# Norm sums in strips of 32 rows, low-rank norms inside the input product, queries rotated per head, attention values for 256 queries at once

## The reference

```python
def rms_norm(x, g):
    xf = x.astype(jnp.float32)
    y = xf * lax.rsqrt(jnp.mean(xf * xf, axis=-1, keepdims=True) + EPS)
    return (y * g.astype(jnp.float32)).astype(x.dtype)
# a layer of the first block, l = 0, 1
hx = modulate(rms_norm(x, norm1_g[l]), sh1, sc1)      # and hc for the context
px = hx @ w_in[l]                                     # 384 q rank, 256 kv rank, 32 rope, 256 fourier, 768 hyena
q  = (rms_norm(px[:, :384], q_norm_g) @ w_uq)         # 8 heads of 64 + 32 (the 32 are rotated by position)
kv = (rms_norm(px[:, 384:640], kv_norm_g) @ w_ukv)    # 8 heads of 64 keys + 64 values
prob = softmax((q_nope k_nope + q_rope k_rope) * scale); o = prob @ v
x = x + g1 * (concat[o, fourier, hyena] @ w_out[l])
x = x + g2 * sq_relu_mlp(modulate(rms_norm(x, norm2_g[l]), sh2, sc2), w_mlp1[l], w_mlp2[l])
```

## Time and profile before

| | us |
|---|---|
| median of 3 runs | 3166.07 (3163.94 to 3166.35) |
| the profiled execution | 3160.84 |
| its span in the trace | 3158.9 |
| mean granted clock of TensorE | 0.946 |
| PE busy | 2836.2 (90%) |
| PE weight loads | 2315.9 (73%) |
| DVE busy | 1645.4 (52%) |
| ACT busy | 1164.0 (37%) |

### The profile page before, as it was taken

The page is one execution under the profiler, slowest core; times in us unless marked ns, Lnnn a source line. Parts: engine busy times, 40 slices in busy tenths (PEclk is TensorE's granted clock), DMA queues, the critical chain, the costliest instruction groups (busy, mean ns, idle before and its releaser), DMA issues.

```text
span 3158.9 us, 43981 instructions
## 1 busy us (share of the span) xinstructions
PE 2836.2 (90%) x16708; PEld 2315.9 (73%) x16708; DVE 1645.4 (52%) x2656; ACT 1164.0 (37%) x2158; POOL 376.3 (12%) x583
## 2 busy tenths in 40 slices
PE   5889789998788897799979999999899986997899
PEld 3636568886646896588758888877688863975799
DVE  3432554334534664587247777774544433358665
ACT  3224242223323543333245445552422223332443
POOL 0000000000000000000026666660000000014000
PEclk8999899999998999899979999999999987999899
DMA  6136122222343455622400000022222247210354
GB/s 245 67 123 237 40 80 93 93 93 80 115 174 129 156 182 224 263 94 95 145 14 1 1 2 1 1 94 84 76 102 98 93 174 275 81 67 1 121 186 146
DMA packets 49600, 343.13 MB, mean 109 GB/s; under 512 B 5296, under 2 KB 7344, under 8 KB 9776
## 3 DMA queue, kind: packets, MB, share of 16 engines
q1 hardware_dynamic: 44960, 324.03, 27.8%
q10 hardware_dynamic: 4496, 17.15, 1.4%
HBM read 333.82 MB, written 7.34 MB: 108 GB/s over the span
## 4 chain that ended last, share of the span: by engine, by line
PE 83%; DVE 7%; ACT 4%; DMA 3%; issue 2%; DVEq 0%; POOL 0%; ACTq 0%; SPq 0%; POOLq 0%
PE ps L514 18%; PE ps L515 18%; PE ps L516 18%; DMA ring<-in_w_dram 3%; PE ps L1848 3%; PE ps L1835 3%; PE ps L1827 2%; PE ps L1856 2%; PE ps L697 1%; PE ps L542 1%; PE ps L689 1%; PE ps L720 1%; PE ps L563 1%; DVE ring_rest L502 1%; PE ps L1790 1%
## 5 line engine op out<-in xcount | busy, mean ns | idle before, releaser
L514 PE MATMUL ps<-hidden_high,w_high 128*128 128x256 f32 (+1 forms) x1160 | 385.5, 332 | 11.8 <-DVE h_rest L510 8.7
L514 PE MATMUL ps<-h_high,w_high 128*128 128x512 f32 (+1 forms) x1024 | 349.2, 341 | 29.9 <-DVE h_low L1377 26.3
L515 PE MATMUL ps<-h_low,w_high 128*128 128x512 f32 (+1 forms) x1024 | 348.0, 340 | 0.0
L999 ACT ACTIVATE w_high<-ring 128x2048 fp32r<-128x2048 f32 x124 | 236.8, 1909 | 295.0 <-PE ps L516 295.0
L515 PE MATMUL ps<-hidden_low,w_high 128*128 128x512 f32 (+1 forms) x1024 | 342.9, 335 | 0.0
L2166 POOL TENSOR_SCALAR RS<-C,arena 128x128 f32<-128x128 f32 x128 | 74.9, 604 | 1635.2 <-DVEq L1750 1635.2
L516 PE MATMUL ps<-hidden_high,ring_rest 128*128 128x256 f32 (+1 forms) x872 | 262.8, 301 | 0.0
L514 PEld LDWEIGHTS ps<-hidden_high,w_high 128*128 128x128 f32 x1160 | 218.2, 188 | 37.0 <-issue 10.7
L514 PEld LDWEIGHTS ps<-h_high,w_high 128*128 128x128 f32 x1024 | 196.0, 191 | 54.4 <-issue 33.0
L1329 DVE SCALAR_TENSOR_TENSOR X<-ps,M,X 128x256 f32<-128x256 f32 x240 | 106.6, 479 | 218.3 <-PE ps L516 218.3
L515 PEld LDWEIGHTS ps<-h_low,w_high 128*128 128x128 f32 x1024 | 196.2, 192 | 20.8
(11 more groups left out here) (400 smaller groups left out, 6312.3 us busy)
## 6 DMA issues: line engine op xcount, KB each, us to landing
ring<-in_w_dram SPq DMA_DIRECT2D x302, 1024.0 KB, 4.8
z_spill<-arena ACTq DMA_DIRECT2D x16, 256.0 KB, 2.0
arena<-z_spill SPq DMA_DIRECT2D x2, 2048.0 KB, 9.6
C<-in_first_dram ACTq DMA_DIRECT2D x1, 2432.0 KB, 8.8
X<-in_x_dram ACTq DMA_DIRECT2D x1, 2048.0 KB, 13.2
x_spill<-X ACTq DMA_DIRECT2D x1, 2048.0 KB, 8.4
X<-x_spill SPq DMA_DIRECT2D x1, 2048.0 KB, 7.6
C<-in_third_dram ACTq DMA_DIRECT2D x1, 2048.0 KB, 14.8
```

Source lines behind the costliest of these rows:

```text
L514: ins = nc.tensor.matmul(out_, w_high, high, start=first, stop=False)
L515: nc.tensor.matmul(out_, w_high, rest, start=False, stop=False)
L999: nc.scalar.activation(W_HIGH[:, (j + 1) % 2, :], ring[:, s], ACT.Copy).then_inc(sems["w_high"], 1)
```

## The change

Five edits:

1. **Sums in strips.** pe_sums no longer multiplies 512 (or 256) columns by 128 x 128 ones. The tokens are cut into four quarters; quarter q is multiplied by 128 x 32 ones in column group q, and its sums land on partitions 32q to 32q+31 of the first T/4 columns of the bank. Root and reciprocal work on 128 x T/4. Then PE spreads the reciprocals back: four matmuls with 32 x 128 ones, one for each strip, into banks 4 to 7 (the ones' 32 rows add 32 equal values, so the root is taken of 1024 times the mean). DVE scales straight from these four banks. In the modulation stages the spread stands behind the last slab.
2. **Low-rank norms within the input product.** The stage is gone. ACT squares the five tiles after its copy of slab 3, PE adds them in strips behind slab 3's filter matmuls, ACT takes two roots after its copy of slab 4, DVE two reciprocals after its copy of slab 4, PE spreads behind slab 4 into banks 0 to 3 (and waits there for both reciprocals), DVE scales the five tiles and rotates the key part after its copy of slab 5. The filter's length moves from tile 14 to 15, and the last slabs' tiles to 13, 20 and 22.
3. **Queries turned per head**: DVE rotates head h as soon as it is out of PSUM, within the query product.
4. **Attention values for 256 queries.** Units go head by head, both query blocks of a head together. DVE takes the reciprocal of each unit's sum and scales its exponentials before they are turned. For each pair of units PE makes one product with the values as weights (128 columns, two heads) and 256 moving columns; DVE copies the 64 rows of the head into MIX. The turning of the output by PE and ACT's copy of it are gone.
5. PT becomes two buffers of 4 x 256, OR is gone, and new small buffers lie in the arena.

```diff
-            nc.tensor.matmul(ps[:, b, 0:T], ones[:], RS[:, 0, 0:T], start=True, stop=False)
-            nc.tensor.matmul(ps[:, b, 0:T], ones[:], square_of(KD - 1)[:, 0:T], start=False, stop=True).then_inc(filled[b], 1)
+            pe_strips(ps[:, b, :], [RS[:, 0, :], square_of(KD - 1)], T).then_inc(filled[b], 1)
+
+        def pe_strips(to, terms, T):
+            w = T // 4
+            for n, x in enumerate(terms):
+                for q in range(4):
+                    ins = nc.tensor.matmul(to[32 * q:32 * q + 32, 0:w], ones[:, 0:32], x[:, q * w:(q + 1) * w], start=(n == 0), stop=(n == len(terms) - 1),
+                                           tile_position=(0, 32 * q))
+            return ins
+
+        def pe_spread(pe, v, x, first, w, nth):
+            for q in range(4):
+                pe.wait_ge(freed[first + q], v.free(first + q, nth[q]))
+                ins = nc.tensor.matmul(ps[:, first + q, 0:w], ones[32 * q:32 * q + 32, :], x[32 * q:32 * q + 32, 0:w], start=True, stop=True)
+            ins.then_inc(sems["spread"], 1)
+
+        def pe_factors(pe, v, nth, T):
+            pe.wait_ge(sems["root"], v.of("root", 1))
+            pe_spread(pe, v, RS[:, 0, :], 4, T // 4, nth)
...
-            nc.scalar.activation(RS[:, 0, 0:T], ps[:, b, 0:T], ACT.Sqrt, bias=eps[:], scale=1.0 / D).then_inc(freed[b], 1)
+            nc.scalar.activation(RS[:, 0, 0:T // 4], ps[:, b, 0:T // 4], ACT.Sqrt, bias=eps32[:], scale=1024.0 / D).then_inc(freed[b], 1)
-            nc.vector.reciprocal(RS[:, 0, 0:T], RS[:, 0, 0:T]).then_inc(dve_step, v.step())
-            dve.wait_ge(dve_step, v.steps())
+            nc.vector.reciprocal(RS[:, 0, 0:T // 4], RS[:, 0, 0:T // 4]).then_inc(sems["root"], 1)
-            nc.vector.tensor_tensor(H[:, k, 0:T], X[:, k, 0:T], RS[:, 0, 0:T], ALU.mult).then_inc(sems["scaled"], 1)
+            if k == 0:
+                dve.wait_ge(sems["spread"], v["spread"])
+            nc.vector.tensor_tensor(quarters(H[:, k, 0:T], T), quarters(X[:, k, 0:T], T), factors(T), ALU.mult).then_inc(sems["scaled"], 1)
...
+        def pe_lora(pe, v, l, j):                      # called after slab j's matmuls and filter
+            if j == 3:
+                b = LORA_SUMS % 8
+                pe.wait_ge(freed[b], v.free(b, LORA_SUMS // 8))
+                pe.wait_ge(sems["squares"], v.of("squares", 5))
+                for n, (first, terms) in enumerate(((0, 3), (3, 2))):
+                    ins = pe_strips(ps[:, b, n * P:n * P + P], [LSQ[:, first + k, :] for k in range(terms)], lora_tokens(l, n))
+                ins.then_inc(filled[b], 1)
+            if j == 4:
+                pe.wait_ge(sems["root"], v.of("root", 3))
...
+            if j == 4:                                 # dve_lora, after the copy of slab 4's second tile
+                nc.vector.reciprocal(LRT[:, 0, 0:T // 4], LRT[:, 0, 0:T // 4]).then_inc(sems["root"], 1)
+                nc.vector.reciprocal(LRT[:, 1, :], LRT[:, 1, :]).then_inc(sems["root"], 1)
...
             for h in range(HEADS):                     # dve_up
-                dve.wait_ge(freed[h], v.freed(h))
-            for h in range(HEADS):
+                if h % 2:
+                    dve.wait_ge(filled[h], v.filled(h))
+                    nc.vector.tensor_scalar(QT[:, h, 0:T], ps[:, h, 0:T], -SCALE, None, ALU.mult).then_inc(freed[h], 1)
+                dve.wait_ge(freed[h], v.freed(h))
                 nc.vector.tensor_tensor(RT[64:96, h, :], QT[96:128, h, 0:L], C[96:128, 0:L], ALU.mult).then_inc(dve_step, v.step())
...
+                if 1 <= i <= n:                        # dve_attn
+                    u = i - 1
+                    dve.wait_ge(freed[u % 2], v.freed(u % 2, u // 2 + 1))
+                    nc.vector.reciprocal(ST[:, 3, u:u + 1], ST[:, 1, u:u + 1]).then_inc(dve_step, v.step())
+                    dve.wait_ge(dve_step, v.steps())
+                    nc.vector.tensor_scalar(PR[:, u % 3, 0:kn], PR[:, u % 3, 0:kn], ST[:, 3, u:u + 1], None, ALU.mult).then_inc(sems["scaled"], 1)
...
+                if 3 <= i < n + 3 and i % 2 == 0:      # pe_attn
+                    s, h, q = units[i - 3]
+                    pair, hp = (i - 4) // 2, h // 2 * P
+                    for a in range(kn // P):
+                        ins = nc.tensor.matmul(ps[:, b, 0:L], VT[:, k0 // P + a, hp:hp + P], PT[:, pair % 2, a, :], start=(a == 0), stop=(a == kn // P - 1))
```

More of the change, by code:

```diff
@@ L316, in build @@
         KA = part(12288, 2, 256)
+        LSQ = part(12800, 5, T2)
+        LRT = part(15360, 2, P)
+        KRT = part(15616, L)
         RK = part(29056, 8)
@@ L618, in pe_filter, with lora_tokens @@
                 ins.then_inc(filled[b], 1)
+        def lora_tokens(l, n):
+            return T2 if l == 0 or n == 1 else L
+        def pe_lora(pe, v, l, j):
[8 more added lines that the diff above has]
+                pe.wait_ge(sems["root"], v.of("root", 3))
+                for n in range(2):
+                    w = lora_tokens(l, n) // 4
+                    for q in range(4):
+                        pe.wait_ge(freed[q], v.free(q, 2))
+                        ins = nc.tensor.matmul(ps[:, q, n * P:n * P + w], ones[32 * q:32 * q + 32, :], LRT[32 * q:32 * q + 32, n, 0:w], start=True, stop=True)
+                    ins.then_inc(sems["spread"], 1)
         def pe_in(pe, v, l):
@@ L625, in pe_in @@
                 pe_filter(pe, v, l, j)
+                pe_lora(pe, v, l, j)
             v.end(U_IN)
[L627 to L631, removed]
-            T = T2 if l == 0 else L
-            for b, (k0, n, tok) in enumerate(((0, 3, T), (3, 2, T2))):
-                pe.wait_ge(freed[b], v.free(b))
-                for k in range(n):
-                    pe.wait_ge(sems["squares"], v.of("squares", k0 + k + 1))
-                    ins = nc.tensor.matmul(ps[:, b, 0:tok], ones[:], H[:, k0 + k, 0:tok], start=(k == 0), stop=(k == n - 1))
-                ins.then_inc(filled[b], 1)
-            v.end(U_LORA)
             pe.drain().then_inc(pe_stage_end, 1)
@@ L925, in act_attn @@
         def act_attn(act, v, l):
-            units, m, through = attn_units(l), len(woven(l)), turned_woven(l)
+            units, m = attn_units(l), len(woven(l))
             n = len(units)
-            for i in range(n + 4):
+            for i in range(n + 2):
                 if i < n:
@@ L1225, in dve_attn, with out_of @@
         def dve_attn(dve, v, l):
-            units, slabs, through = attn_units(l), woven(l), turned_woven(l)
+            units, slabs = attn_units(l), woven(l)
             n, m = len(units), len(slabs)
-            for i in range(n + 3):
+            def out_of(pair):
+                s, h, q = units[2 * pair]
+                b, r = 4 + pair % 2, 64 * (h % 2)
+                dve.wait_ge(filled[b], v.filled(b, pair // 2))
+                nc.vector.tensor_copy(MIX[r:r + 64, h // 2, s * L:(s + 1) * L], ps[r:r + 64, b, 0:L]).then_inc(freed[b], 1)
+            for i in range(n + 4):
                 if i < n:
@@ L1416, in build @@
         U_READ = {**{b: 3 for b in (2, 3, 4, 6)}, 7: 2, 5: 2, "h_high": 16, "h_split": 16}
-        U_DOUT = {**banks(9), "slab": 8, **U_SUMS, "w_high": 8, "w_split": 8}
+        U_DOUT = {**banks(9), "spread": 1, "root": 1, "slab": 8, **U_SUMS, "w_high": 8, "w_split": 8}
         DIRS = (0, 1)
```

202 lines of the change are left out of this document (89 added, 113 removed).

## The result

The changed kernel takes 3084.99 us (median of four executions, 3075.03 to 3090.59) against 3165.59 us before: ratio 0.9749, 95% interval 0.9728 to 0.9771, 80.6 us less. A second comparison gave 3084.17 against 3163.86 us, 0.9749 with 0.9736 to 0.9762. The forecast was 3097.6 us with a range of 3082 to 3116: sign and range hold, the size was 12.6 us too small.

The account below looks back on a forecast made before the run. PE was taken as the bound (busy 2836 of 3158.9 us), gains being its pauses and low clock. Terms -33.2 + 9.2 - 4.0 - 22.4 - 14.5 - 3.5 = -68.4 from 3160.84 gave 3092.4, as median 3097.6; range 3082 to 3116.

Parts of the forecast that it names:

- Low-rank stage gone, work put into the input product: Between input and query product: removing the norms' own stage gains 33.2 us in two layers; their work inside costs 9.2.
- the wait behind slab 4: Input product: PE waits for DVE's copy and two reciprocals before slab 5, costing 2.0 us in layer 0, 1.3 in layer 1.
- Clock behind it: Query product: without the long pause before it PE keeps its clock, -4.0 us over two layers (bounds 0 and -5).
- Rotation: Query rotation hidden beside the query product: attention starts 10.0 us earlier per layer, plus 1.2 of clock each, together -22.4.
- The 1.3 us a head for PE in layer 1: Layer 1 query product: PE needs 1.3 us a head, so DVE's rotation falls back a few us and catches up later.
- Nine norms: Block norms in strips: shorter sums, roots and reciprocals less a new spread, -14.5 us in all (bounds -5 and -19).
- The spread's 0.75: Block norms: PE's eight instructions spreading the reciprocals back were taken at 0.75 us, between 1.0 one by one and 0.35 overlapped.
- the first rival: Spreads overlap in row groups (0.35 instead of 0.75 us) and strips are cheap (1.3): 3092 us, chance 0.2.
- Attention: Attention stage: turning gone (-3.4), values product +0.2 a layer, small gains and costs at the ends, sum -3.5 (bounds -7 and +5).
- attention steps over 4 us: Attention: a sign that would show the prediction wrong; right would be steps of 3.5 us with no 4.5 among them.
- +1.0 for the units and -1.0 for the tail: Layer 0's attention end: last eight units without a slab cost 1.0 us for DVE's work; the shorter tail gains 1.0.
- the fourth rival, attention as a chain: Attention: PE's transposes wait for DVE's minimum, reciprocal and scaling, 1.6 us in each of 48 units, +77, so 3174; chance 0.03.

Follow-up runs that it names:

- the best one: Changed kernel plus value products of two heads at a time, low-rank reciprocals ahead of slab 4's copy and an early one-column root: 3062.87 us, ratio 0.9684.
- the head pairs: Changed kernel with value products of two heads at a time, each with 64 weight columns in its own column half: 3075.52 us, ratio 0.9722.

## Why the prediction was right, and where it was off

- *Low-rank stage gone, work put into the input product* (-33.2 + 9.2 = -24.0): measured -24.8. Terms inside were off and cancel. The spreads and strips are cheaper than put (0.66 and 1.2 us in layer 0, against 1.2 and 1.7), and the wait behind slab 4 was 1.67 us against 2.0: slab 5 starts 66.0 us behind the stage's first product where it was 62.8, 3.3 us later instead of 4.9. But in eight of nine profiles the clock falls behind that wait, which the sum had at 0: 1.6 us in slabs 5 and 6.
- *Clock behind it* (-4.0): -4.5, the windows at 1.00 instead of 0.59.
- *Rotation* (-22.4): -19.95 and 1.9 of clock. The hand-over of 0.15 us was right. The 1.3 us a head for PE in layer 1 is not what the earlier trace rows give (12.83 / 8 = 1.6, part of it at the low clock); the changed kernel's 10.53 us for eight heads bear it out.
- *Nine norms* (-14.5): the seven on the path gave -19.0 by stages, where they were put at -15.3; undoing the nine cost 15.5 by medians. This is the mis-sized term. The start gained 4.9 against 4.0, the one behind layer 0's output product 3.0 against 2.7, the two of 512 tokens behind MLP and delta 3.35 and 3.42 against 3.1, the three of 256 tokens 4.4 against 2.4 together. From the start of the reciprocal to the first scale the seven gave 8.8 us, where the sum had 13.2 for the reciprocals less seven times 0.85 for spread and hand-over, some 7.2. The spread's 0.75 was too dear: it took 0.45 to 0.51 at the full clock, though 0.69 to 0.81 where the clock was low. The rest of the excess lies in the sums: from the first sum to the root the 256-token norms took 1.1 to 2.1 us in the kernel before, the longer ones at least in part at the low clock, and 0.5 to 1.2 with strips. On the spread the first rival was right, at a chance of 0.2; its 3092 was still 7 us high.
- *Attention* (-3.5): 1.2 to 1.35 by stages, nothing by medians. The turning went as said. The sign "attention steps over 4 us" came up and meant no harm: with one product for two units the steps are 2.66 and 4.40 us, 3.53 on average. Half of what is missing is in the last eight units of layer 0: from the first of their scores to the Fourier stage 15.97 us before, 17.1 now (256.18 to 273.25), where +1.0 for the units and -1.0 for the tail had been put. There two units take 3.0 us, 1.5 each where they took 1.3, and no engine is busy throughout:

```profile
261.14 0.43 DVE L1257 COPY arena<-ps 64x256 f32<-64x256 f32 x1 [0.91 <-PE ps L751]
261.60 0.42 DVE L1264 TENSOR_REDUCE arena<-ps 128x1 f32<-128x256 f32 x1
261.94 0.15 DVE L1269 RECIPROCAL arena<-arena 128x1 f32<-128x1 f32 x1
262.13 0.35 DVE L1271 TENSOR_SCALAR arena<-arena 128x256 f32<-128x256 f32 x1
262.40 0.42 DVE L1264 TENSOR_REDUCE arena<-ps 128x1 f32<-128x256 f32 x1
...
264.18 0.41 DVE L1257 COPY arena<-ps 64x256 f32<-64x256 f32 x1 [0.91 <-PE ps L751]
```

  DVE waits 0.91 us for PE's product before it copies, and then scales the exponentials of the next unit, for which PE waits in turn (0.41 to 0.87 us, L740). This is the fourth rival, attention as a chain, in the eight units that have no slab to fill PE's steps; elsewhere it did not come. The other half, some 0.6 us in layer 1 and the rest in layer 0, was not located.
- *What the sum did not have*: 13.4 us outside its terms. 4.4 are the two Fourier stages, where the kernel before starts at the low level and the changed one at the full one:

```profile
273.20:278.20 5.00, 4.95 (x23) 4.41 (x24) 0.00 (x0) 2.39 (x4) 0.00 (x0) 1.00 0.02 3
```
```profile
306.10:311.10 5.00, 4.98 (x12) 3.96 (x13) 0.00 (x0) 1.20 (x2) 0.00 (x0) 0.50 0.00 0
```

  The first is the changed kernel, the second the kernel before in its second profile. In layer 1 no single undoing brings the slow stage back (7.8 us, 6.3 with the edits), so it hangs on more than one of the edits, and which is open. All twelve profiles with edits bear out 1.5 us in layer 1, and at least 0.9 in layer 0 (12.9 at most, 13.8 at least before). The other 9 us lie in the convolution (39.4 to 43.4 us with the same code), in the last modulation, where PE waits for the weights' DMAs (72 to 81), and the like. With two profiles of the kernel before they cannot be told from the spread of single executions.

So the mechanism held. The stages of the edits gave 71.5 us, where the same terms of the sum make 69.2. What the sum left out is that the clock can change elsewhere too, in stages without an edit and behind a wait that the change itself puts in; of the former at least 2.4 us is shown. Some 9 us of the profiles' difference is tied to no edit. The measured median lies 3 us inside the range and single executions lie below it, so that the range held is in part luck.

## What to carry to other kernels

Divide the span at PE's first instruction of each stage and compare two profiles of each kernel: here that shows an effect of 0.5 us in a stage whose clock does not vary, where five executions leave one of 4 us open. Look at the clock first: with the same code, the input product of layer 1 took 63.4 or 64.9 us, the convolution 39.4 to 43.4. Where one engine waits for a serial chain of a few small instructions, price the clock behind the pause as well as the pause; a 1.7 us pause cost 1.6 us more of matmuls at the low level in most profiles, and a pause of 1.0 us did so in one of nine. And a matmul that leaves half of its output columns unused has a neighbour that could run beside it.

## What the runs showed of the hardware that was not expected

- Four matmuls of 32 rows (eight instructions) take 0.50 us in four row groups and 1.15 in one at a granted clock of 1.00, 0.81 and 2.07 at 0.50; two column groups of 64 nearly double the rate of 256-column matmuls (sixteen in 1.95, eight in 1.89).
- The same pauses ahead of a stage don't always give the same clock. Ahead of layer 1's Fourier stage PE pauses for 1.02 and then for 0.72 us both in the kernel before and in the one with only attention undone, with the same instructions there; the stage took 7.79 us in the one and 6.29 in the other. And the pause of 1.67 us behind slab 4 was followed by the low level in eight profiles and by the full clock in one.
- Delta's input products are 288.0 and 289.0 us in the two kernels that have one more tile of one column beside the small constants, and 291.9 to 294.5 in the twelve others. The stage's end is at the low level in all of them, but they already differ ahead of it: from PE's 100th to its 1000th instruction the stage takes 204.0 us in those two and 208.0 to 209.0 in the others, at a granted clock of 1.00. In the same window, also at 1.00, of the changed kernel and of the best one there are 432 and 443 matmuls:

```profile
1300.00:1400.00 100.00, 100.00 (x432) 80.88 (x431) 81.91 (x99) 36.33 (x45) 0.00 (x0) 1.00 0.27 95
```
```profile
1300.00:1400.00 100.00, 100.00 (x443) 82.79 (x442) 82.49 (x101) 37.36 (x47) 0.00 (x0) 1.00 0.26 95
```

  The tile moves the addresses of everything allocated behind it; that this is the cause is argued, not shown. It is half of what the best version gains over the head pairs.
